# A tuned two-block transformer on one core: low parts of two norm chunks on VectorE in place of GpSimd, and sums, pooled parts, modulation units and an output chunk at other places of TensorE's order

## The reference

```
layer 0: x += gate * mixer(modulate(rms(x)));  x += gate * relu(modulate(rms(x)) @ w1)^2 @ w2   (ctx likewise)
layer 1: q, k, v from modulate(rms(x)), k, v of the context too; windowed attention with a bias; @ na_w_out;
         x += gate * relu(modulate(rms(x)) @ w1)^2 @ w2
```

## Time and profile before

| | |
|---|---|
| median of three executions | 1355.67 us |
| the profiled execution's own time | 1354.78 us |
| its span | 1352.6 us |
| TensorE busy | 1318.6 us |
| VectorE busy | 826.3 us |
| ScalarE busy | 595.3 us |
| GpSimd busy | 433.4 us |

### The profile page before, as it was taken

How to read it: one execution, slowest core, us unless ns; L and a number is a source line. 1 busy time by engine, 2 the same in 40 slices (tenths; PEclk the granted TensorE clock), 3 DMA queues, 4 the chain that set the end, 5 groups by cost and what they waited for, 6 DMA issues and landing times.

```text
span 1352.6 us, 19992 instructions
## 1 busy us (share of the span) xinstructions
PE 1318.6 (97%) x7852; PEld 1115.1 (82%) x7852; DVE 826.3 (61%) x1265; ACT 595.3 (44%) x953; POOL 433.4 (32%) x432
## 2 busy tenths in 40 slices
PE   9999999999999999979999999999799999999999
PEld 8888888899886788768788888787577777999987
DVE  6687678899776445369544444334467766855553
ACT  5336546566563223244321234222445553766432
POOL 2352132233420001265400144111556552388300
PEclk9999999999999999989999999999899999999999
DMA  7786367845455222344434333345423221555552
GB/s 288 264 280 235 142 210 277 300 181 182 162 189 193 78 94 79 111 153 160 167 128 152 143 140 140 140 142 185 161 89 108 93 84 45 187 188 181 188 191 79
DMA packets 63965, 220.08 MB, mean 163 GB/s; under 512 B 6913, under 2 KB 10241, under 8 KB 63873
## 3 DMA queue, kind: packets, MB, share of 16 engines
q1 hardware_dynamic: 63584, 218.56, 45.9%
q10 hardware_dynamic: 288, 0.25, 0.1%
HBM read 217.73 MB, written 1.05 MB: 162 GB/s over the span
## 4 chain that ended last, share of the span: by engine, by line
PE 89%; DVE 4%; POOL 3%; issue 2%; ACT 1%; DMA 1%; SPq 0%; DVEq 0%; POOLq 0%; ACTq 0%
PE ps L551 22%; PE ps L565 22%; PE ps L563 22%; PE ps L541 7%; PE ps L543 4%; PE ps L629 2%; POOL xn L2280 2%; PE ps L957 1%; PE ps L984 1%; PE ps L971 1%; DVE wlo L1537 1%; PE ps L595 1%; PE ps L950 1%; POOL ssum_c L2189 1%; DMA R<-in_x 1%
## 5 line engine op out<-in xcount | busy, mean ns | idle before, releaser
L551 PE MATMUL ps<-A,whi 128*128 128x256 f32 (+2 forms) x1580 | 519.3, 329 | 2.4 <-ACT A L1318 1.7
L565 PE MATMUL ps<-A,wlo 128*128 128x256 f32 (+2 forms) x1552 | 495.7, 319 | 0.1
L563 PE MATMUL ps<-A,whi 128*128 128x256 f32 (+2 forms) x1552 | 495.4, 319 | 0.0
L1537 DVE TENSOR_TENSOR wlo<-raw,whi 128x1024 fp32r<-128x1024 f32 x305 | 393.1, 1292 | 100.4 <-ACT whi L1077 100.1
L1077 ACT ACTIVATE whi<-raw 128x1024 fp32r<-128x1024 f32 x305 | 319.8, 1051 | 289.8 <-PE ps L565 163.0
L551 PEld LDWEIGHTS ps<-A,whi 128*128 128x128 f32 x1580 | 300.2, 190 | 55.9 <-issue 27.9
L563 PEld LDWEIGHTS ps<-A,whi 128*128 128x128 f32 x1552 | 295.2, 190 | 22.3 <-issue 1.9
L565 PEld LDWEIGHTS ps<-A,wlo 128*128 128x128 f32 x1552 | 294.7, 190 | 21.2 <-DVE wlo L1537 0.4
L541 PE MATMUL ps<-H,whi 128*128 128x512 f32 x432 | 151.4, 394 | 0.0
L2178 POOL TENSOR_TENSOR H<-tmp,H 128x256 fp32r<-128x256 f32 (+1 forms) x86 | 123.9, 1440 | 63.8 <-ACT H L1372 45.8
L543 PE MATMUL ps<-H,wlo 128*128 128x256 f32 x432 | 121.4, 281 | 0.0
(11 more groups left out here) (282 smaller groups left out, 1461.1 us busy)
## 6 DMA issues: line engine op xcount, KB each, us to landing
raw<-in_ada SPq DMA_DIRECT2D x96, 512.0 KB, 4.3
raw<-in_w SPq DMA_DIRECT2D x64, 512.0 KB, 3.4
raw<-in_w_up SPq DMA_DIRECT2D x44, 512.0 KB, 4.2
raw<-in_w_in SPq DMA_DIRECT2D x38, 512.0 KB, 5.5
raw<-in_w_0a SPq DMA_DIRECT2D x32, 512.0 KB, 3.6
raw<-in_w_0b SPq DMA_DIRECT2D x32, 512.0 KB, 3.4
raw<-in_na_in SPq DMA_DIRECT2D x24, 512.0 KB, 5.3
raw<-in_w_down SPq DMA_DIRECT2D x22, 512.0 KB, 3.4
```

Of the source, the lines that this page charges most:

```text
L551: e.matmul(o, w_hi, ah, start=k == 0, stop=False)
L563: e.matmul(o, w_hi, al, start=False, stop=False)
L565: m = e.matmul(o, w_lo, ah, start=False, stop=last)
L1537: e.tensor_tensor(wlo[i % NRAW][:, :cols], raw[i % NRAW][:, :cols], plain(whi[s % NHI][:, :cols]), SUB).then_inc(S("wlo").sem, 1)
```

## The change

`LOW_P` goes from three chunks to two: at both shifted norms GpSimd makes the low parts of chunks 0 and 1, VectorE those of 2 to 7. Four modulation units move from behind units of `w_up` to the front of `ab_in`, four of whose ten are loaded ahead of its first two weight units; two of them are taken between the sums of the tokens' norm, whose order is changed. The context's sum of squares moves from unit 4 to unit 5 of `w_down`. The pooled parts come one chunk earlier in `w_in`; their signal is counted by itself. The sum of the last VectorE-made modulation units goes ahead of `na_in`'s first chunks, its turning one chunk later. Chunk 3 of `na_out` is made like the first three, in bank 4, behind the last attention product; its low weight is split one unit earlier, and the last values are turned in the middle of chunk 0.

```diff
--- before.py
+++ after.py
@@ -45,19 +45,19 @@
 
 
 ADA_STEPS = 96
-ADA_BEFORE = {"ab_in": 6, "w1_0a": 6, "na_in": 8}
-
-AHEAD = {"w1_0a": 3, "na_in": 3}
-
-LOW_P = range(3)
-ADA_AFTER = {"w_in": (6, 22), "w_out": (0, 48), "w_up": (2, 42)}
+ADA_BEFORE = {"ab_in": 10, "w1_0a": 6, "na_in": 8}
+
+AHEAD = {"ab_in": 4, "w1_0a": 3, "na_in": 3}
+
+LOW_P = range(2)
+ADA_AFTER = {"w_in": (6, 22), "w_out": (0, 48), "w_up": (2, 38)}
 
 
 MOD = range(54, 88)
 MOD_AFTER = ("w1_0a", "w2_0a", "w1_0b", "w2_0b")
-MOD_SUMMED = {("w1_0a", 15): 3, ("w1_0b", 15): 4, ("na_in", 1): 5}
-
-ADA_WRITTEN = {("w_in", 34): 0, ("w_up", 6): 1, ("ab_in", 2): 2, ("w2_0a", 1): 3, ("w2_0b", 1): 4, ("na_in", 3): 5}
+MOD_SUMMED = {("w1_0a", 15): 3, ("w1_0b", 15): 4, ("na_in", 0): 5}
+
+ADA_WRITTEN = {("w_in", 34): 0, ("w_up", 6): 1, ("ab_in", 2): 2, ("w2_0a", 1): 3, ("w2_0b", 1): 4, ("na_in", 4): 5}
 
 EARLY = {"w_in": 38, "w_up": 44, "w1_1": 32}
 
@@ -74,7 +74,7 @@
 TURNED = {27 + h: h for h in range(8)}
 VALUES = {29 + 2 * p: p for p in range(4)}
 
-POOLED_AT = {36: (0, 1), 37: (2, 3)}
+POOLED_AT = {35: (0, 1), 36: (2, 3)}
 
 
 NA_CHUNKS = [(x[0], int(x[1])) for x in ("k0 q0 v0 k1 q1 k2 q2 v1 k3 q3 k4 q4 v2 k5 q5 v3 k6 q6 v4 k7 q7 v5 v6 v7").split()]
@@ -167,7 +167,7 @@
         hi[i] = range(n_hi, max(n_hi, upto))
         n_hi = max(n_hi, upto)
 
-        behind = 0 if e + 1 < len(TAKEN) and any(TAKEN[e + 1] == FRONT[x][0] for x in AHEAD) else 1
+        behind = 0 if PLAN[i] == ("na_out", 0) or e + 1 < len(TAKEN) and any(TAKEN[e + 1] == FRONT[x][0] for x in AHEAD) else 1
         ahead = max(n_hi - behind, sum(TAKEN_AT[at] <= e for at in SPLIT))
         lo[i] = range(n_lo, max(n_lo, ahead))
         n_lo = max(n_lo, ahead)
@@ -212,8 +212,8 @@
                  ("d1_r", 8)],
     "normed": [("nc_t", 8), ("n2_t", 8), ("m0_t", 16), ("na_t", 16)],
     "norm_hi": [("nc_hi", 8), ("n2_hi", 8), ("m0_hi", 16), ("na_hi", 16)],
-    "norm_lo": [("nc_lo", 8), ("n2_lo", 8), ("m0_lo", 10), ("na_lo", 10)],
-    "norm_lo_p": [("m0_lp", 6), ("na_lp", 6)],
+    "norm_lo": [("nc_lo", 8), ("n2_lo", 8), ("m0_lo", 12), ("na_lo", 12)],
+    "norm_lo_p": [("m0_lp", 4), ("na_lp", 4)],
     "early_hi": [("e0_hi", 8), ("e1_hi", 8), ("e2_hi", 8)],
     "early_lo": [("e0_lo", 8), ("e1_lo", 8), ("e2_lo", 8)],
     "square": [("n1_sq", 8), ("nx_sq", 8), ("m0_sq", 8), ("na_sq", 8), ("m1_sq", 8)],
@@ -229,7 +229,7 @@
     "hidden_hi": [("H_hi", 22), ("h0a_hi", 16), ("h0b_hi", 16), ("h1_hi", 32)],
     "hidden_lo": [("H_lo", 22), ("h0a_lo", 16), ("h0b_lo", 16), ("h1_lo", 32)],
     "rescaled": [("resc_w_in", 38), ("resc_w_up", 44), ("resc_w1_1", 32)],
-    "input_hi": [("O_hi", 4), ("B_hi", 4), ("mix_hi", 4), ("Z_hi", 8), ("C_hi", 4), ("D_hi", 4), ("O2_hi", 8)],
+    "input_hi": [("O_hi", 4), ("mix_hi", 4), ("Z_hi", 8), ("C_hi", 4), ("D_hi", 4), ("O2_hi", 8)],
     "input_lo_v": [("O_lo", 4), ("mix_lo", 4), ("D_lo", 4)],
     "input_lo": [("B_lo", 4), ("Z_lo", 8), ("C_lo", 4), ("O2_lo", 8)],
 }
@@ -855,13 +855,21 @@
                following=lambda u: ada_following("w_up", u))
 
         def after_down(u):
-            if u == 4:
+            if u == 5:
                 row_sum(ps[4][:, :256], ssum_c, X[0][:, 256:512], "nc_part", 6, "nc_sq", 8, "nc_sum")
 
         linear("w_down", 256, lambda k: Hc(k, 256), ready("H_hi"), ready("H_lo"), following=after_down, both=lambda k: H2[:, k])
-        row_sum(ps[5][:, :256], ssum[:, :256], sq[0][:, :256], "nx_part", 6, "nx_sq", 8, "nx_sum")
+
+        w.wait_ge(S("nx_part"), 6)
+        e.matmul(ps[5][:, :256], const("ones"), ssum[:, :256], start=True, stop=False)
         w.wait_ge(S("nc_v"), 1)
-        row_sum(ps[4][:, :256], ssum_g, sq[1][:, :256], "ng_part", 6, "ng_sq", 8, "ng_sum")
+        w.wait_ge(S("ng_part"), 6)
+        e.matmul(ps[4][:, :256], const("ones"), ssum_g, start=True, stop=False)
+        ada_before("ab_in", 0, 2)
+        w.wait_ge(S("nx_sq"), 8)
+        e.matmul(ps[5][:, :256], const("ones"), sq[0][:, :256], start=False, stop=True).then_inc(S("nx_sum").sem, 1)
+        w.wait_ge(S("ng_sq"), 8)
+        e.matmul(ps[4][:, :256], const("ones"), sq[1][:, :256], start=False, stop=True).then_inc(S("ng_sum").sem, 1)
 
 
         def during_ab(n):
@@ -888,7 +896,7 @@
             w.wait_ge(S("nc_lo"), k + 1)
             w.wait_ge(S("n2_lo"), k + 1)
 
-        ada_before("ab_in")
+        ada_before("ab_in", 2)
         linear("ab_in", 512, lambda k: (Ahi[:, k], Alo[:, k]), n2_hi, n2_lo, during=during_ab)
         w.wait_ge(S("ab_yt"), 16)
         for c in range(4):
@@ -934,6 +942,7 @@
         ada_before("na_in", 4, 6)
         column_rows("na")
         ada_before("na_in", 6)
+        mod_summed("na_in", 0)
 
         def turn_bank(what, j):
 
@@ -1020,6 +1029,9 @@
             g, s = CHUNK_AT["na_out", n], SPLIT_AT["na_out", n]
             o = ps[g % 3][:, :256]
             signal, count = bank_left(*CHUNKS[g - 3])
+            if n == 3:
+
+                o, signal, count = ps[4][:, :256], "na_bank", len(turn2)
             w.wait_ge(S(signal), count)
             w.wait_ge(S("whi"), s + 1)
             low_ready(s)
@@ -1037,16 +1049,19 @@
 
         for u in range(23, LAST2 + 1):
             after_na(u)
-            if u < 26:
+            if u == 23:
+                out_part(0, range(3))
+                during_na(24)
+                out_part(0, range(3, 6))
+            elif u < 26:
                 out_part(u - 23, range(6))
-            if u == 23:
-                during_na(24)
             if u == 26:
                 for n in range(3):
                     out_part(n, (6,))
-        for n in range(3):
+        out_part(3, range(7))
+        for n in range(4):
             out_part(n, (7,))
-        linear("na_out", 256, lambda k: (Ohi[:, k], Olo[:, k]), ready("O2_hi"), ready("O2_lo"), begin=3)
+        linear("na_out", 256, lambda k: (Ohi[:, k], Olo[:, k]), ready("O2_hi"), ready("O2_lo"), begin=4)
 
         def during_1(n):
             if n == 0:
@@ -1082,7 +1097,7 @@
 
         def product(name, n):
             w.wait_ge(S("mm"), CHUNK_DONE[name, n])
-            return ps[CHUNK_AT[name, n] % 3]
+            return ps[4] if (name, n) == ("na_out", 3) else ps[CHUNK_AT[name, n] % 3]
 
         def early_hi(st, into, c, cols, gain):
             e.activation(into[:, c, :cols.stop - cols.start], R[:, c, cols], ACT.Copy, scale=gain).then_inc(S(st + "_hi").sem, 1)
```

## The result

The changed kernel takes 1333.22 us (median of four runs, 1332.03 to 1335.21) against 1354.70 us before (four runs, 1352.75 to 1355.76): a ratio of 0.9845, 95% interval 0.9825 to 0.9864. 1330.2 us was forecast, with a range of 1326.5 to 1335.5. The profiled execution took 1334.13 us with a span of 1332.1 us, 20.5 us less than before, where the sum of terms said 25.5.

A forecast was written before the change was run, and what follows sets the result against it. TensorE, busy 1318.6 of 1352.6 us, was taken as the bound, so only its stops and the clock lost behind them could go. Terms of 8.7 + 8.7 + 1.0 + 3.8 + 2.4 + 0.3 + 0.6 + 0 = 25.5 us gave 1330.2 us, range 1326.5 to 1335.5.

The forecast's parts named there:

- The norms: Both shifted norms: moving chunk 2's low parts to VectorE, with the modulation sum ahead at the second, saves 8.7 us each.
- the rival in which the operation ahead of it is caught: At the norms, GpSimd's last operation of chunk 1 is held instead, giving 1338 or 1344 us; chance 0.08.
- The VectorE run of 12 as the new bound: First norm: VectorE makes 12 low parts in place of 10, 0.404 us apart, the last ready at 586.21.
- The modulation sum and the turning: Second norm: eight small sum passes (1.06 us) move ahead, inside its 8.7 us; turning a chunk later saves 1.0 us.
- The up-projection: Four modulation units leave it; two pairs at 1.19 us each save 2.4 us on TensorE's path.
- The context's sum: Down-projection: a unit later, the 2.1 us wait for GpSimd and the half clock behind go, saving 3.8 us.
- The front of the mixer: Mixer's first product: ten units stand where TensorE waits anyway, saving 0.3 us; bounds -0.6 and +1.0.
- The pooled parts: Pool product: a chunk earlier, ScalarE's two copies no longer delay the pool weight's high part, saving 0.6 us.
- half clock elsewhere, or a wait that only moves: Rival: two half-clock stretches behind short stops, or one and a late ada load, give 1333 to 1334 us; chance 0.14.
- Near 996 us: Existing stretch of 3.41 us at clock 0.50, behind matmuls with short waits; a stretch like it costs 1.7 us.
- The fourth chunk of the output product: Attention's output product: fills the last attention chunk's wait, but the fifth chunk waits instead; 0, bounds -1 and +1.
- the signs named for being wrong: A 6 us GpSimd operation, ScalarE or TensorE waiting for modulation-unit or mixer-weight loads, or clock 0.50 behind a short stop.

The follow-up runs named there:

- two runs: Changed kernel with GpSimd's third low-part chunk given back at both norms: span 1346.3 us; the same plus a wait holding VectorE until GpSimd finishes: 1335.2 us.
- the kernel with three chunks: Changed kernel with three chunks of the attention's output product begun ahead in place of four: that stage 39.03 us, with a half-clock stretch inside.

## Why the prediction was right, and where it was wrong

**The bound** was read rightly: TensorE's stops and its clock behind them were all that could go. Its idle time in the list shrank, its busy time fell from 1318.6 to 1313.1 us for the same 7852 passes, and no other engine became the bound.

**The norms** carried 17.4 of 25.5 us, and 17.2 came. The third chunk alone is worth 14.8 us of that, as the run that gives it back shows (8.1 and 6.7 us). Both the held operation and its cause are now shown by two runs, and the rival in which the operation ahead of it is caught did not occur in any profile: with one or two chunks GpSimd's longest operation there was 0.75 us. The VectorE run of 12 as the new bound was right to 0.1 us.

**The modulation sum and the turning** were right: 2.25 us when undone, of which the ledger had 1.06 inside the norm and 1.0 at the turning.

**The up-projection** gave 2.36 for 2.4 us.

**The context's sum** was worth 3.1 us for 3.8. The step "the 2.1 us go" took no account of what a stop leaves behind it: the six chunks behind take 7.77 us each in place of 7.63, which gives 0.9 us back. The other part, the half clock, was there in the profile before, but the experiment with the old place shows that it is not there in each execution; without it the move is worth 1.3 us.

**The front of the mixer** is the step that failed: the last unit's load "lands 4.3 us later, 421.9; TensorE has until 422.7 before the chunk ends later, so this is hidden with 0.8 us to spare". VectorE's chain did gain its 0.3 us. Two terms of it were too small. I let the load go at TensorE's start on the third unit, but it went out 1.1 us behind that start (413.31 and 414.41). And 4.3 us is the median of all 96 such loads; the last of the ten, issued behind two others, took 5.8 us. Three waits came of it. The part cost 2.7 us where I had -0.3 with a bound of +1.0. The trace of before could have warned me: there five loads of the mixer's weights, issued 0.5 to 0.7 us apart from 419.17 us on, landed 1.3 to 1.4 us apart, the first 4.3 us and the last 7.5 us behind its issue.

**The pooled parts** gave their 0.6 us. The half clock behind them stood among the rivals ("half clock elsewhere, or a wait that only moves") and took 1.67 us in the profiled execution.

**Near 996 us** the reverse happened: I kept that half clock in the sum, and it was gone in the profiles after but for one. It gives 1.6 us, of which the scores behind it take 0.5 back. In the kernel with the old place of the context's sum it was back, at 975.5 us, so its absence is no merit of the change.

**The fourth chunk of the output product** was costed at 0 and cost 0.4 us, inside its bounds (0.6 by the kernel with three chunks). The 0.43 us that I expected its earlier split to put on the last turning are not seen: the scores take as long without it. I had the wait of the fifth chunk for its weight's low part; ahead of it stands the one for VectorE's residual (1.4 us), which I had named as work on VectorE's queue, not as what frees the bank.

Put together: 25.5 - 0.2 (norms) - 0.2 (turning) - 0.7 (sum) - 3.0 (mixer) - 0.4 (tail) + 1.1 (near 996) = 22.1 us, and less 1.67 for one half-clock stretch the 20.5 us of the profiled execution. The measured time lies inside the range, but the case that came is the second rival, half clock elsewhere and late loads of modulation units (1333 to 1334 us, chance 0.14), and not the forecast's own (0.71): the median is 1333.22 us, and two of the signs named for being wrong are there, TensorE's waits for these loads and a granted clock of 0.50 behind a stop of 1.7 us. The late loads are in every execution profiled, the half clock in some. The range was wide enough because it took that rival in. And in part it is luck: the absence of the half clock near 996 us, worth 1.1 us, is no work of the change. Against the 25.5 us forecast the medians differ by 21.5 us.

## What to carry to other kernels

Where GpSimd helps VectorE, look at what VectorE does in the meantime. Beside a run of low parts and splits, which read two tiles, a GpSimd operation of 0.7 us waited to the end of the run; beside a run of scaling operations, which read one, it was not touched. So finish the short helper work before such a run begins, or leave it out. Only this direction was seen, and only with these operations. Loads that become possible together do not land together; for work moved into a wait, ask when the last of its loads lands, with all that is issued in the same microseconds. And where half-clock stretches fall by chance, compare stage by stage: a difference of 2 us between two spans may be one stretch more.

## What the runs showed that was not expected

- The same stop of 1.74 us was followed by a half-clock stretch of 3.4 us in five profiles of twelve, and the stop of 1.44 us at the fifth output chunk in five of ten. The Trainium skill (TensorE: Matmul & The Clock Gate, "What's actually happening") says that the number of slow passes at a kernel's start differs from run to run; here the same holds in mid-kernel.
- One profile had such a stretch at 975.5 us, where the longest wait of TensorE in the 20 us ahead was 0.7 us: in this case a stretch came without a stop of a microsecond. Another had one at 10.7 us, behind a wait of 1.9 us for the first weights.
- A product of 22 pairs of passes a chunk takes 7.77 us when it has run on without a stop, and 7.63 us behind a stop, even one of 0.16 us, at the same granted clock of 1.00; whether the stop or the place of the sum sets it is open.
- Loads of 512 KB, the second issued 0.37 us behind the first and the third 1.7 us behind that, landed 1.8 to 2.0 us apart in the execution shown, and 1.3 to 2.0 us apart in the ten profiles with ten units. An estimate by the fit in the Trainium skill (DMA: Bandwidth & Descriptors, "Anatomy of one DMA — SWDGE (gpsimd) path"), made for GpSimd's queue, whose part that grows with size is bytes / 436e3, would put them 1.2 us apart; the shortest measured, 1.3 us, comes near it, the others are longer, and the measurement decides.
